# Expert passes of a MoE layer on one core: gathering, selection copies and the adding of the last result moved between gates and ups, results kept as 128 rows in two parts

## The reference, cut to what matters

```
g_prob = softmax(h @ w_rg + b_rg);  g_top, g_idx = top_k(g_prob, 1)        # 1 of 4 groups
e_prob = softmax(e_logits of that group); e_top, e_idx = top_k(e_prob, 2)  # 2 of 8 experts
e_w = e_top / sum(e_top) * g_top
combine = sum(one_hot(flat_idx, 32) * e_w)                                 # (256, 32)
a = einsum('sd,edf->sef', hs, w_gate)      # 32 experts, 1024 -> 256
u = einsum('sd,edf->sef', hs, w_up)
act = silu(a) * u * combine
x = x + einsum('sef,efd->sd', act, w_down) # 256 -> 1024
return rms_norm(x, norm_final_g)
```

## Time and profile before

| | before |
|---|---|
| median of 3 runs | 383.27 us (383.26 to 384.05) |
| span of the profiled execution | 382.1 us |
| own time of that execution | not listed beside its span; the median is 1.2 us above the span |
| PE busy | 315.4 us (83%) |
| DVE busy | 173.1 us (45%) |
| ACT busy | 129.6 us (34%) |
| moved by transfers | 121.68 MB, mean 318 GB/s |
| passes 0 to 17 | 171.1 to 370.4 us |

### The profile page before, as it was taken

How to read it: one execution, slowest core, us unless ns; L and a number is a source line. 1 busy time by engine, 2 the same in 40 slices (tenths; PEclk the granted TensorE clock), 3 DMA queues, 4 the chain that set the end, 5 groups by cost and what they waited for, 6 DMA issues and landing times.

```text
span 382.1 us, 11483 instructions
## 1 busy us (share of the span) xinstructions
PE 315.4 (83%) x4700; PEld 242.2 (63%) x4701; DVE 173.1 (45%) x473; ACT 129.6 (34%) x294; POOL 37.9 (10%) x57
## 2 busy tenths in 40 slices
PE   2799999999998799449969897989999978576581
PEld 2699989798863445137657665767666646456350
DVE  3726374653453425974434443345444442242234
ACT  4748174444353336722202222222222221120133
POOL 0200001632303012720000000000000000000001
PEclk9899999999999899969989999899999998898986
DMA  8999750173579282867999999999999999999922
GB/s 275 368 387 387 283 229 0 34 298 124 208 295 402 49 342 94 335 264 304 416 416 361 418 418 415 416 412 422 417 416 420 417 418 420 411 425 413 417 85 110
DMA packets 31434, 121.68 MB, mean 318 GB/s; under 512 B 5432, under 2 KB 7760, under 8 KB 23216
## 3 DMA queue, kind: packets, MB, share of 16 engines
q1 hardware_dynamic: 28608, 119.94, 79.1%
q10 hardware_dynamic: 2800, 1.36, 1.3%
HBM read 120.24 MB, written 1.05 MB: 317 GB/s over the span
## 4 chain that ended last, share of the span: by engine, by line
PE 56%; SPq 14%; DMA 7%; issue 7%; DVE 6%; ACT 6%; DVEq 3%; ACTq 1%; POOLq 0%
PE bank L434 12%; SPq L324 9%; PE bank L428 7%; PE bank L499 6%; DMA ring<-in_w_up_dram 6%; PE bank L703 6%; PE bank L645 6%; SPq L331 5%; PE bank L682 5%; PE bank L655 3%; PE bank L448 2%; PE bank L463 1%; ACT yb L970 1%; PE bank L692 1%; PE bank L473 1%
## 5 line engine op out<-in xcount | busy, mean ns | idle before, releaser
L682 PE MATMUL bank<-ring,hT 128*32 128x128 f32 x2240 | 72.2, 284 | 21.8 <-DMA ring<-in_w_up_dram 12.3
L682 PEld LDWEIGHTS bank<-ring,hT 128*32 128x32 f32 x2240 | 66.3, 115 | 36.8 <-issue 31.9
L1370 DVE SCALAR_TENSOR_TENSOR yb<-bank,pp,yb 64x512 fp32r<-64x512 f32 x36 | 27.0, 749 | 46.9 <-ACT yb L970 46.4
L645 PE MATMUL bank<-pp,qk 128*128 128x64 bf16 x912 | 33.2, 200 | 11.5 <-DVE pp L1303 7.8
L645 PEld LDWEIGHTS bank<-pp,qk 128*128 128x128 bf16 x912 | 30.7, 103 | 16.5 <-DVE pp L1303 10.9
L1113 DVE TENSOR_TENSOR unit_lo<-ring,unit_hi 128x2048 fp32r<-128x2048 f32 (+1 forms) x12 | 26.3, 2206 | 30.8 <-ACT unit_hi L777 30.8
L703 PE MATMUL bank<-ring,pp 128*32 128x512 f32 x280 | 35.1, 605 | 0.0
L970 ACT ACTIVATE yb<-bank,pp 64x512 fp32r<-64x512 f32 x36 | 24.6, 683 | 29.2 <-PE bank L703 28.8
L499 PE MATMUL bank<-ring,qk 128*128 128x512 f32 x64 | 30.7, 622 | 0.0
L960 ACT ACTIVATE pp<-bank 128x128 f32<-128x128 f32 x18 | 5.0, 277 | 72.4 <-PE bank L682 72.4
L655 PE MATMUL bank<-yb,selT 128*128 128x512 f32 x76 | 24.3, 443 | 1.7 <-DVE yb L1370 1.6
(11 more groups left out here) (201 smaller groups left out, 453.0 us busy)
## 6 DMA issues: line engine op xcount, KB each, us to landing
ring<-in_w_gate_dram SPq DMA_DIRECT2D x31, 1024.0 KB, 14.6
ring<-in_w_up_dram SPq DMA_DIRECT2D x31, 1024.0 KB, 17.9
ring<-in_w_down_dram SPq DMA_DIRECT2D x31, 1024.0 KB, 16.4
ring<-in_w_in_dram SPq DMA_DIRECT2D x5, 2048.0 KB, 20.1
ring<-in_w_out_dram SPq DMA_DIRECT2D x1, 4096.0 KB, 12.6
ring<-in_w_in_dram SPq DMA_DIRECT2D x2, 1024.0 KB, 7.3
work<-in_x_dram SPq DMA_DIRECT2D x2, 512.0 KB, 4.0
work<-in_w_up_dram SPq DMA_DIRECT2D x1, 1024.0 KB, 4.9
```

What stands on the lines that cost most here:

```text
L645: last = mm(p_hg[:, k * CP:(k + 1) * CP], hs[:, i, t, k, :], selb[:, t, :], start=(t == 0 and i == 0), stop=(t == NT - 1 and i == 2))
L682: last = mm(p_gu[b:b + CAP, w * P:(w + 1) * P], hg[:, k, CAP * e:CAP * (e + 1)], w_gu[at[e]][:, w, k, h, :], start=(k == 0), stop=(k == KD ...
L1370: V.scalar_tensor_tensor(out=yb[half][rest, :], in0=p_y[rows, :], scalar=wcol[rows, :], in1=yb[half][rows, :].bitcast(fp32), op0=ALU.mult, ...
```

## The change

- In a pass on the matrix engine the order is now: gates; the selection turned round and the weight column; the adding of the last result; the gathering for the next pass; ups; the activation turned round; downs.
- The result tile is no longer split by columns. `y_hi` and `y_lo` hold the high and the low part of all 128 rows of `p_y` (rows 0 to 63 the left half of the columns, 64 to 127 the right half). ACT writes `y_hi` in one instruction and DVE `y_lo` in one, where there were two and two.
- `add_back` is called for `y_hi` and for `y_lo`. Each call issues four matmuls of 64 rows by 512 columns, rows 0 to 63 and 64 to 127 in turn, into different banks: eight a pass for four before.
- ACT copies the weight column and `selT` at the start of its pass; DVE's program keeps its order.
- After the last pass the banks are finished by `y_lo`, so their order is left, right, left, right.

```diff
@@ -201,8 +201,8 @@
         hg = hTf[:, 0:HALF].rearrange("p (k c) -> p k c", k=KD)
 
 
-        yb = [nc.alloc_sbuf_tensor_at(f"yb{h}", [P, HALF], f32r, offset=hT_at + 4 * a)
-              for h, a in enumerate((HALF, 2 * HALF + SEQ))]
+        y_hi, y_lo = (nc.alloc_sbuf_tensor_at(n, [P, HALF], f32r, offset=hT_at + 4 * a)
+                      for n, a in (("y_hi", HALF), ("y_lo", 2 * HALF + SEQ)))
         selT = nc.alloc_sbuf_tensor_at("selT", [P, SEQ], f32r, offset=hT_at + 4 * 2 * HALF)
         M0 = NT * D
         selw = pp[:, M0:M0 + NT * P].rearrange("p (t c) -> p t c", t=NT)
...
@@ -649,12 +649,14 @@
             def gather_signalled():
                 gather().then_inc(gathered, 1)
 
-            def add_back(half, final=False):
+            def add_back(y, final=False):
 
                 for t in range(NT):
-                    last = mm(acc[t][half][:, :], selT[:, t * P:(t + 1) * P], yb[half][:, :], start=False, stop=final)
-                    if final:
-                        last.then_inc(acc_done, 1)
+                    for half in range(2):
+                        rows = slice(CP * half, CP * (half + 1))
+                        last = mm(acc[t][half][:, :], selT[rows, t * P:(t + 1) * P], y[rows, :], start=False, stop=final)
+                        if final:
+                            last.then_inc(acc_done, 1)
                 return last
 
             pe.wait_ge(sel_ready, 1)
...
@@ -662,17 +664,18 @@
 
             def add_result(i):
 
-                pe.wait_ge(y_ready, 2 * i + 1)
-                add_back(0)
-                pe.wait_ge(y_ready, 2 * i + 2)
-                add_back(1).then_inc(added, 1)
+                pe.wait_ge(y_hi_ready, i + 1)
+                add_back(y_hi)
+                pe.wait_ge(y_ready, i + 1)
+                add_back(y_lo).then_inc(added, 1)
 
             def one_pass(i, at, loaded):
 
 
 
                 pe.wait_ge(hg_ready, i + 1)
-                for w in range(2):
+
+                def gate_or_up(w):
                     for e in range(2):
                         pe.wait_ge((gate_in, up_in)[w][at[e]], loaded[e] * 16)
                     for k in range(KD):
...
@@ -682,17 +685,21 @@
                                 last = mm(p_gu[b:b + CAP, w * P:(w + 1) * P], hg[:, k, CAP * e:CAP * (e + 1)], w_gu[at[e]][:, w, k, h, :],
                                           start=(k == 0), stop=(k == KD - 1))
                     last.then_inc((gate_done, gu_done)[w], 1)
-                pe.wait_ge(sel_ready, i + 2)
-                gather_signalled()
+
+                gate_or_up(0)
                 pe.wait_ge(selT_ready, i + 1)
                 pe.wait_ge(selw_ready, i + 1)
                 for t in range(NT):
                     mm(p_tr[:, t * P:(t + 1) * P], selo[:, t, :], identb, start=True, stop=True)
                 for t in range(NT):
-                    mm(p_tr[:, 3 * P:3 * P + 1], selw[:, t, :], onescol, start=(t == 0), stop=(t == NT - 1))
+                    last = mm(p_tr[:, 3 * P:3 * P + 1], selw[:, t, :], onescol, start=(t == 0), stop=(t == NT - 1))
+                last.then_inc(seltr_done, 1)
+                add_result(i)
+                pe.wait_ge(sel_ready, i + 2)
+                gather_signalled()
+                gate_or_up(1)
                 pe.wait_ge(act_ready, i + 1)
                 nc.tensor.transpose(p_tr[:, 2 * P:3 * P], act_sb, ident).then_inc(actt_done, 1)
-                add_result(i)
                 pe.wait_ge(actT_ready, i + 1)
                 for e in range(2):
                     pe.wait_ge(dn_in[at[e]], loaded[e] * 16)
...
@@ -720,9 +727,10 @@
                     couple(g * TURN + (FIRST + j), places(FIRST + j), (g + 2, g + (3 if j == TURN - 1 else 2)))
             passes_all = pe.value_load(base[0:1, COUPLES:COUPLES + 1], min_val=COUPLES, max_val=ITEMS_MAX)
             pe.wait_ge(selT_ready, passes_all + 1)
-            for half in range(2):
-                pe.wait_ge(y_ready, passes_all * 2 + (half + 1))
-                add_back(half, final=True)
+            pe.wait_ge(y_hi_ready, passes_all + 1)
+            add_back(y_hi)
+            pe.wait_ge(y_ready, passes_all + 1)
+            add_back(y_lo, final=True)
 
 
         @block.scalar
...
@@ -956,18 +964,17 @@
             act.dma_start(gfin, I["norm_final_g"].rearrange("(o d) -> o d", o=1).to_broadcast([P, D])).then_inc(gfin_in, 16)
 
             def one_pass(i):
+                act.wait_ge(seltr_done, i + 1)
+                act.wait_ge(added, i + 1)
+                nc.scalar.copy(wcol, p_tr[:, 3 * P:3 * P + 1]).then_inc(wcol_ready, 1)
+                nc.scalar.copy(selT[:, :], p_tr[:, 0:SEQ]).then_inc(selT_ready, 1)
                 act.wait_ge(gu_done, i + 1)
                 A(sig, p_gu[:, 0:P], ACT.Sigmoid).then_inc(sig_ready, 1)
                 act.wait_ge(actt_done, i + 1)
                 nc.scalar.copy(actT, p_tr[:, 2 * P:3 * P]).then_inc(actT_ready, 1)
-                nc.scalar.copy(wcol, p_tr[:, 3 * P:3 * P + 1]).then_inc(wcol_ready, 1)
-                act.wait_ge(added, i + 1)
-                nc.scalar.copy(selT[:, :], p_tr[:, 0:SEQ]).then_inc(selT_ready, 1)
                 act.wait_ge(wcol_ready, i + 1)
                 act.wait_ge(down_done, i + 1)
-                for half in range(2):
-                    rows = slice(CP * half, CP * (half + 1))
-                    A(yb[half][rows, :], p_y[rows, :], ACT.Copy, scale=wcol[rows, :]).then_inc(y_hi_ready, 1)
+                A(y_hi[:, :], p_y[:, :], ACT.Copy, scale=wcol).then_inc(y_hi_ready, 1)
 
 
             act.wait_ge(base_ready, 1)
...
@@ -977,7 +984,7 @@
             load_table(ACT.Sqrt)
 
             for t, half in ((0, 0), (0, 1), (1, 1)):
-                act.wait_ge(acc_done, NT * half + t + 1)
+                act.wait_ge(acc_done, NT * t + half + 1)
                 last = A(outb[t][:, half * HALF:(half + 1) * HALF], acc[t][half][:, :], ACT.Square,
                          accum_out=ssq4[:, t, half:half + 1])
             last.then_inc(ssq_ready, 1)
...
@@ -1364,11 +1371,9 @@
                 dve.wait_ge(actt_done, i + 1)
                 weigh(at_next, i + 1)
                 dve.wait_ge(wcol_ready, i + 1)
-                for half in range(2):
-                    dve.wait_ge(y_hi_ready, 2 * i + (half + 1))
-                    rows, rest = slice(CP * half, CP * (half + 1)), slice(CP * (1 - half), CP * (2 - half))
-                    V.scalar_tensor_tensor(out=yb[half][rest, :], in0=p_y[rows, :], scalar=wcol[rows, :],
-                                           in1=yb[half][rows, :].bitcast(fp32), op0=ALU.mult, op1=ALU.subtract).then_inc(y_ready, 1)
+                dve.wait_ge(y_hi_ready, i + 2)
+                V.scalar_tensor_tensor(out=y_lo[:, :], in0=p_y[:, :], scalar=wcol, in1=y_hi[:, :].bitcast(fp32),
+                                       op0=ALU.mult, op1=ALU.subtract).then_inc(y_ready, 1)
 
             def couple(q):
                 first = dve.value_load(base[0:1, bass.ds(q, 1)], min_val=0, max_val=ITEMS_MAX)
...
@@ -1389,7 +1394,7 @@
                 dve.wait_ge(dve_step, passes_all * STEPS + (steps0 + n))
 
 
-            dve.wait_ge(acc_done, 2)
+            dve.wait_ge(acc_done, 3)
             V.tensor_copy(outb[1][:, 0:HALF], acc[1][0][:, :]).then_inc(dve_step, 1)
             own(1)
             V.scalar_tensor_tensor(out=outb[1][:, 0:HALF], in0=outb[1][:, 0:HALF], scalar=1.0, in1=acc[1][0][:, :],
```

More of the change, by code:

```diff
@@ L270, in layer_program @@
             sem(n) for n in ("actT_ready", "down_done", "y_hi_ready", "y_ready", "added"))
-        wcol_ready = sem("wcol_ready")
+        wcol_ready, seltr_done = sem("wcol_ready"), sem("seltr_done")
         acc_set, acc_done, fin_ready = sem("acc_set"), sem("acc_done"), sem("fin_ready")
@@ L1064, in _ @@
             nc.gpsimd.memset(selT[:, :].bitcast(fp32), 0.0).then_inc(selT_ready, 1)
-            for half in range(2):
-                nc.gpsimd.memset(yb[half][:, :].bitcast(fp32), 0.0).then_inc(y_ready, 1)
+            nc.gpsimd.memset(y_hi[:, :].bitcast(fp32), 0.0).then_inc(y_hi_ready, 1)
+            nc.gpsimd.memset(y_lo[:, :].bitcast(fp32), 0.0).then_inc(y_ready, 1)
             pool.wait_ge(gfin_in, 16)
```

## The result

The changed kernel is slower, by less than half of what was forecast: median 386.31 us (382.55 to 387.69, 7 runs) for 383.27 (381.98 to 384.57, 7 runs) before, ratio 1.007 with the interval 1.0037 to 1.0103. Forecast were 389.9 and a range of 384.0 to 393.5; the direction and the range held, the size did not. The profiled execution has a span of 384.5 us for 382.1. Each ratio is taken with runs of the kernel before that stand beside that kernel's own, and leaves out as slow what lies over 1.5% above its kernel's fastest run, which is four of the twelve runs with late filling and no other.

A forecast was written before the change was run, and what follows sets the result against it. The weight stream bound the kernel, the chain of passes having 1.16 us a pass of slack. The lengthened chain would lead: span 382.1 + 7.2 - 0.55 = 388.7, median 389.9 us, range 384.0 to 393.5.

The forecast's parts named there:

- The pass: Gates to next gates: 11.04 us for 9.64, +1.40; passes that had not waited for the selection +2.13, to 10.80.
- pairs overlapping: In the adding, the two row halves run together, so eight matmuls of 64 rows take 1.13 us.
- The sum over passes 0 to 13: Three passes at +2.13 and eleven at +1.40 make +21.8 us, so pass 13 ends at 332.8.
- The stops I leave as they are: PE's stops on first walks through the unrolled code (2.05 us in pass 2) and the half clock behind them stay.
- the cover: If the new bare stretch between ups and downs hides PE's stops, it gives back up to 4 us.
- The end: Last four passes at chain pace, 44.8 us; downs end at 377.6, +7.2, the chain leading the weight loads by 2 us.
- Behind the last downs: From the last downs' end to ACT's first square: 2.5 us for 3.05, so -0.55.
- the 1.2 us from span to median: Added to the forecast span of 388.7 us, since the median lay 1.2 above the profile's span, giving 389.9.
- Stream still leads: Rival: the last weight loads set the end if a pass grows by under 1.16 us; 384.3 us, chance 0.16.
- No overlap: Rival: the row halves in the adding run one after another, 2.0 us, a pass 11.67; 402 us, chance 0.08.
- a falling clock in the bare stretch: Rival: PE drops to half clock between ups and downs; +5 us if in a third of passes, no separate chance.
- Faster: Rival: the moved work fills PE's idle wait for ups in the last four passes; 380.8 us, chance 0.07.

The follow-up runs named there:

- late filling: The kernel before with 48 idle matmuls between gates and ups in passes 5 to 17; 384.44 us, ratio 1.0008.
- two experiments on the gathering: The changed kernel with the gathering moved back behind the ups, 381.98 us; and the same with its last 12 matmuls behind the turned activation, 381.38 us.
- split gathering: The changed kernel with the gathering behind the ups and its last 12 of 48 matmuls behind the turned activation; 381.38 us, ratio 0.9962.
- form alone: The changed kernel with its new result form but the old order of the pass and of ACT's copies; 382.18 us, ratio 0.9983.
- both filled ones: The kernel before with 48 idle matmuls between gates and ups, in passes 0 to 3 (388.57 us) or in passes 5 to 17 (384.44 us).
- many short: The changed kernel with 34 idle bf16 matmuls of 64 columns (68 instructions) behind the ups; 392.61 us, ratio 1.0243.
- order alone: The kernel before with the new order on the matrix engine and the old result form; 393.90 us, ratio 1.0298.
- few long: The changed kernel with two idle float32 matmuls of 256 columns (8 instructions) behind the ups; 385.21 us, ratio 1.0058.

## Why the prediction was wrong

- *The pass.* Right in each term: 11.07 for 11.04, a first pass of 10.75 for 10.80, pass 3 10.71; 0.28 of waiting for the selection, pairs overlapping, 1.74 bare for 1.81. The two experiments on the gathering confirm where the cost sits.
- *The sum over passes 0 to 13.* Wrong. Forecast were +21.8, measured +16.2. The failing step is the sentence "The stops I leave as they are". They fell from 5.3 to 0.9 us, and the half clock behind two of them went too. Passes 2 and 6 together, forecast at +2.8, came out at -2.9 (13.18 to 11.79, 13.02 to 11.50): of these 5.7, 2.8 are stops and some 3 the half clock. That is all of the missing 5.6; the rest cancels, for passes 4 and 7 grew by less than the forecast 1.40 (0.72 and 1.20) and passes 8 and 12 by more (1.78 and 1.91). The text gave the cover "up to 4 us" as an aside and had it as a condition of one rival, but it had no part in the forecast.
- *The end.* Forecast: the chain sets the end, 2 us behind the stream. With a chain 5.6 shorter it is the reverse at the last step: pass 3's gates came 1.9 later and not 4.9, no pass waited for ups, and the last downs waited 0.84 for their own loads and lost another 0.88 at half clock. The last four passes took 46.3 for the forecast 44.8. So the sum is 16.2 + 46.3 - 59.4 = +3.1 for +7.2 (the last four took 59.4 before). The forecast looked at the landing of the ups alone and not at that of the downs, which come two loads, some 5 us, after them; by its own numbers the downs would have landed near 374.8, 0.9 ahead of the chain and not 2.
- *Behind the last downs.* 2.58 for 2.5. And one small slip: the 1.2 us from span to median came from a median and the span of another execution. Every run that lists both has its time some 1.8 above its own span (386.31 for 384.5), so the forecast span of 388.7 stood for 390.5, further off by 0.6.
- *The rivals.* "Stream still leads" (384.3) had the mechanism that won in part, with stops hidden as its condition; it was given 0.16. That the measured time lies inside the range is partly luck: the range was built for a chain without that term. No overlap and a falling clock in the bare stretch are ruled out by the rows above. Faster did not come, though one of seven runs of the change took 382.55.

The change was costly at one place: it took the gathering away from beside the activation's chain. The rest of it together, the form and the turning and adding ahead of the ups, gains with the split gathering (0.9962). That the turning and adding gain anything beyond the form is not shown: with the form alone the ratio is 0.9983, and the intervals overlap.

## What to carry to other kernels

Where an engine has to wait for two others, leave it work that nobody needs yet; and put into the time ahead of a transfer only what no later step would have covered. Before adding up a change, ask what the new waits do to the idle times that have no releaser: here a pass without stops got 1.4 to 2.1 us longer, and a quarter of the forecast growth (5.6 of 21.8) did not come, because the engine no longer outran its instructions. With two clocks, a chain and a stream, find the point where the one hands its delay to the other (here the gates of the third couple's second pass); of 4.4 us ahead of it all was handed on, and 16.0 behind it cost at most 2. When executions of different kernels are compared stage by stage, look first whether the clock was at the same level.

## What the runs showed of the hardware

- PE stops within a row of matmuls on the first walk through a couple's code, 0.3 to 2.6 us at a time, and goes on 2.2 to 2.6 us after the start of a 16 KB block on the instruction queue (34 of 34 stops). The kernels that keep it supplied with short matmuls have 5.3 to 8.2 us of stops (before, form alone, both filled ones, many short); the two gathering kernels, with the bare stretch filled again but the new order, 2.6 and 2.8; those with a stretch of some 1.7 us a pass that holds few instructions 0 to 0.9 (the change, order alone, few long). None came after pass 7, when the loop's code is walked again, though the stream was as full as before.
- A change of the array's tiling shape costs 0.07 to 0.10 us at full clock: before, L655 to L703 0.33 for 0.23 within L655; in the change, L695 to L657 0.18 for 0.11 within L695. Six a pass for two stand in the pass's 11.07. The Trainium skill, TensorEngine Tiling (Array Packing), Key Properties, has the drain without a price; the trace agrees.
- 1.05 us idle, a turning and 0.35 more, in every pass, kept the clock at full speed in all 17 passes of the changed kernel that wait for no load; in pass 2 before, idles of 0.87 and 2.05 with 0.38 of work between them were followed by half clock.
- Behind the idle ahead of pass 0 the clock rose at 168.9 to 170.6 us in five executions and at 172.5 to 179.3 in five, the latter with PE already busy in pass 0; the half clock there took up to 4.1 us.
